# The opening of a two-block transformer kernel: x's tiles loaded back to back, the band matrix in halves, and another order of the pool products

## The chip, the core and the metric

One core of one Trainium2 chip runs the whole program. The metric is the device time of one execution in microseconds, as the median of several executions. Three executions of the kernel before are shown. One further execution of it was profiled.

## The reference, cut to what matters

The model takes 256 tokens of width 1024 through two blocks in float32. The change touches only the very first step of it:

```python
h = rms_norm(x, norm_mix[0])
x = x + pool_mixer(h, pool_w[0], pool_scale[0])
h = rms_norm(x, norm_ffn[0])
x = x + swiglu(h, ffn_w_gate[0], ffn_w_up[0], ffn_w_down[0])
...
```

The pool mixer takes, in each of four groups of 256 columns, the mean over the last 2, 4, 8 or 16 tokens less the token itself, multiplies it by that group's 256x256 matrix of pool_w, and scales the columns by pool_scale. Behind it come a gated feed-forward net (FFN), an attention layer with its own FFN, and a second, longer block. None of these is edited.

## The kernel before, in words

**Layout.** Tokens lie on partitions in two tiles of 128 (t = 0, 1), the width of 1024 in eight slices of 128 (k = 0 to 7). A product that has to be exact to float32 is made from three faster ones: each operand is split into a high part (rounded to float32r, made by ScalarE) and a low part (what is left, made by VectorE as value minus high part), and TensorE sums high by high, high by low and low by high. Weight blocks go round through three buffers, `raw` as loaded, `wh` high and `wl` low.

**Engines.** The program is written by hand, one instruction stream per engine, with semaphores between them. There is no scheduler: each stream runs strictly in the order of the code. SyncE (SP) issues nearly all DMAs, on one queue. GpSimd (POOL) makes the small reciprocal roots and issues a few DMAs much later (cw1, L1785, then cw2, the small bsc and others behind it on its queue; the last gain, L1824, alone).

**The opening, stage by stage.**
- SP issues x's first tile (L526), the band matrix (L528), pool_scale (L529), x's second tile (L526), the table of column gains `col` (L530), pool_w in two halves (L533), `con` and the positions (L535, L536), and then the weights of the FFN (L499).
- TensorE meanwhile multiplies zeros, `WARM_PRODUCTS` = 8 times (L2058, two records each), then spreads pool_scale over all partitions by a product with ones (L2063).
- ScalarE squares x in halves of 512 columns (L722, via `square`), POOL makes the reciprocal root of each tile (L1730, L1731), and VectorE scales the band matrix by it: one instruction for t = 0 (L1265), two for t = 1 (L1269, L1270).
- TensorE makes the pooled and turned activations, all eight slices of t = 0 and then all of t = 1 (L2075). The pooling is itself a product with the band matrix. Three products of zeros follow (`WARM_POOL`, L2081).
- VectorE scales pool_w in two halves (L1279). ScalarE makes the high parts of the turned slices and of pool_w: slices 0, 1, lower half of the weight, slices 2, 3, upper half, slices 4 to 7, then `hi(1)`, the high part of the first FFN block (L731 to L737).
- VectorE makes the low parts: slices 0 to 3 (L1281, recorded at L1091), lower half of the weight (L1283), slices 4 to 7. The low part of the upper half of the weight is POOL's (L1749).
- TensorE's pool products (L2092 to L2115): the lower half's high products, `pool_pass` with xl for both tiles, then with the low weight. For the upper half all three passes of t = 0 come first, then all three of t = 1.
- VectorE adds the four results to x (L1299) in the order n = 0 to 3. Behind n = 1 and n = 2 it makes a quarter of the low part of the first FFN block (`first_quarter`, L1290). The other two quarters come behind `normalise(1)`.
- ScalarE squares the new x (L722), POOL makes the roots, ScalarE scales tile 0 (L616), VectorE tile 1 (L1109), TensorE turns both (L1852) after three more products of zeros (`WARM_BETWEEN`, L2117), and the first product of the FFN begins (`first_up`, L1951).

The order of the work around the change is therefore set by the order of the code on each engine, by the order of SP's one queue, and by the semaphores `x_tile`, `band_loaded`, `pool_scaled`, `t_hi`, `t_lo`, `pool_lo`, `lo_done` and `bank_sum`.

Of the kernel before, what the change touches and what calls it, by code (L numbers as in the profile page):

```python
# [18 lines left out]
ALU = mybir.AluOpType  # L19
AX = mybir.AxisListType  # L20

P = 128
# [44 lines left out]
WARM_PRODUCTS, WARM_POOL, WARM_BETWEEN = 8, 3, 3  # L67
# [44 lines left out]
NBAND = FRONT + NG * EDGE  # L112
NPOOL = FRONT + NG * P


def constants():
# [23 lines left out]
    bands[:, :FRONT] = full[:, :P, :P + EDGE].transpose(1, 0, 2).reshape(P, -1)  # L140
    bands[:, FRONT:] = full[:, P:, P:P + EDGE].transpose(1, 0, 2).reshape(P, -1)
# [94 lines left out]
def build(nc, w, consts, bands, columns_in, positions_in, out):  # L236
# [17 lines left out]
    with ExitStack() as ctx:  # L254
# [147 lines left out]
        con_loaded, band_loaded = sem("con_loaded"), sem("band_loaded")  # L402
# [72 lines left out]
        def _(sp):  # L475
# [93 lines left out]
        def _(act):  # L569
# [150 lines left out]

            def square(q, n, src, t, c):
# [345 lines left out]
        def _(dve):  # L1067
# [192 lines left out]
            def by_group(ap):  # L1260
                return ap.rearrange("p (g c) -> p g c", g=NG)
# [6 lines left out]
            second_tile = by_group(bandr[:, FRONT:NPOOL])  # L1268
            dve.tensor_scalar(second_tile[:, :, 0:EDGE], by_group(band[:, FRONT:NBAND]), rstd[:, 0, 1:2], None, ALU.mult)  # L1269
            dve.tensor_scalar(second_tile[:, :, EDGE:P], by_group(band[:, 0:FRONT])[:, :, EDGE:P], rstd[:, 0, 1:2], None,  # L1270
                              ALU.mult).then_inc(pool_scaled, 1)

# [8 lines left out]
            split_t(0, xh, xl, C_MIX0, 0, range(4))  # L1281
# [3 lines left out]
            split_t(0, xh, xl, C_MIX0, 0, range(4, 8), 4)  # L1285
# [7 lines left out]
            for n, (t, c) in enumerate(((0, 0), (1, 0), (0, 1), (1, 1))):  # L1293
# [424 lines left out]
        def _(pool):  # L1718
# [24 lines left out]

            then(pool.memset(mhalf[:, :], -0.5))

            pool.memset(ksw[:, :, :, :], 0.0).then_inc(ksw_zero, 1)
            inverse_rms(0)
# [84 lines left out]
        def _(pe):  # L1832
# [252 lines left out]
            def pool_pass(half, t, a, b, start=False):  # L2085
                for k in range(4 * half, 4 * half + 4):
# [18 lines left out]

# [488 lines left out]
```

## Time and profile before

| | |
|---|---|
| median of 3 executions | 898.56 us (896.94, 898.56, 898.69) |
| the profiled execution, whole | 898.74 us |
| its span from first to last instruction | 896.8 us |
| TensorE busy | 882.8 us, 98% of the span |
| VectorE busy | 674.3 us, 75% |
| ScalarE busy | 479.6 us, 53% |
| POOL busy | 54.6 us, 6% |
| DMA | 153.47 MB, mean 171 GB/s |

The span leaves out 1.9 us of the profiled execution's own time, before the first and after the last instruction. TensorE is busy nearly all the time, so the time of the whole is TensorE's work plus the few microseconds in which it waits. In the opening, however, part of what TensorE does is multiplying zeros, and there it is a record of busy time that computes nothing.

### The profile page before, as it was taken

What the parts mean: (1) busy time and instruction counts of PE and PEld (TensorE: products, weight loads), DVE (VectorE), ACT (ScalarE), POOL (GpSimd) and SP (SyncE); (2) the same over time, 40 slices, a digit from 0 to 9 for tenths busy, and PEclk for the clock granted to TensorE, in tenths of its full rate; (3) what the DMA queues carried; (4) which work ended last, traced back from release to release, by engine and by line L of the source; (5) the groups of instructions that cost most, each with busy time, mean ns of one, the idle gap of its engine ahead of it and who ended that gap; (6) DMA issues with size and microseconds to landing.
All of it is one profiled execution on the core that took longest, in us unless ns stands there. A gap on an engine that the chain in (4) does not pass through costs nothing.

```text
span 896.8 us, 14483 instructions
## 1 busy us (share of the span) xinstructions
PE 882.8 (98%) x5258; PEld 783.0 (87%) x5258; DVE 674.3 (75%) x1015; ACT 479.6 (53%) x750; POOL 54.6 (6%) x93
## 2 busy tenths in 40 slices
PE   9999999999999999999999999999999899999996
PEld 7888888889998888888888999998998888888885
DVE  5787767778646588677677788896643799999997
ACT  6654444466555665344444645556544665556554
POOL 3300000020000000000000500001100000000000
PEclk9999999999999999999999999999999999999999
DMA  8987666552532768666546684312553566676531
GB/s 248 301 241 210 198 177 186 164 175 84 165 141 94 208 172 255 176 200 197 178 140 211 158 256 156 109 48 73 188 179 101 165 188 187 189 211 185 178 106 47
DMA packets 185574, 153.47 MB, mean 171 GB/s; under 512 B 5089, under 2 KB 170593, under 8 KB 185522
## 3 DMA queue, kind: packets, MB, share of 16 engines
q1 hardware_dynamic: 184770, 150.36, 55.4%
q0 software_dynamic: 752, 2.39, 1.0%
q8 instruction: 35, 0.57, 0.3%
q14 instruction: 17, 0.14, 0.1%
HBM read 151.17 MB, written 1.05 MB: 170 GB/s over the span
## 4 chain that ended last, share of the span: by engine, by line
PE 92%; ACT 3%; DVE 3%; issue 1%; POOLq 0%; POOL 0%; ACTq 0%; DVEq 0%
PE bank L1980 26%; PE bank L1986 13%; PE bank L1835 13%; PE bank L1837 13%; PE bank L1836 13%; PE bank L1951 2%; PE bank L1852 2%; PE bank L1940 1%; DVE wl L1082 1%; ACT wh L588 1%; PE bank L2325 1%; PE bank L2348 1%; PE bank L2529 1%; PE bank L2058 1%; PE bank L2335 1%
## 5 line engine op out<-in xcount | busy, mean ns | idle before, releaser
L1980 PE MATMUL bank<-xhl,wh 128*128 128x512 f32 x1008 | 240.2, 390 | 0.0
L1980 PEld LDWEIGHTS bank<-xhl,wh 128*128 128x128 f32 x1008 | 188.9, 188 | 40.8
L1986 PEld LDWEIGHTS bank<-xhl,wl 128*128 128x128 f32 x1008 | 129.3, 191 | 4.9
L1986 PE MATMUL bank<-xhl,wl 128*128 128x256 f32 x1008 | 130.6, 283 | 0.0
L1221 DVE TENSOR_TENSOR wl<-raw,wh 128x2048 fp32r<-128x2048 f32 x57 | 130.1, 2282 | 0.2 <-ACT wh L674 0.2
L1082 DVE TENSOR_TENSOR wl<-raw,wh 128x2048 fp32r<-128x2048 f32 (+3 forms) x50 | 104.5, 2099 | 28.4 <-ACT wh L588 28.3
L674 ACT ACTIVATE wh<-raw 128x2048 fp32r<-128x2048 f32 x57 | 108.7, 1907 | 3.3 <-DMA raw<-in_ffn_w_up 3.0
L1837 PE MATMUL bank<-dh,hl 128*128 128x512 f32 x264 | 103.4, 392 | 0.0
L1836 PE MATMUL bank<-dl,hh 128*128 128x512 f32 x264 | 103.1, 390 | 0.0
L1835 PE MATMUL bank<-dh,hh 128*128 128x512 f32 x264 | 102.9, 390 | 0.1
L588 ACT ACTIVATE wh<-raw 128x2048 fp32r<-128x2048 f32 (+3 forms) x51 | 89.5, 1769 | 18.1 <-PE bank L1837 7.2
L1170 DVE TENSOR_REDUCE gs<-bank 128x256 f32<-128x512 f32 x66 | 45.4, 687 | 54.6 <-PE bank L1986 54.6
L1213 DVE TENSOR_TENSOR dl<-draw,dh 128x1024 fp32r<-128x1024 f32 x66 | 80.4, 1219 | 4.3 <-ACT dh L650 4.3
L664 ACT ACTIVATE th<-gs 128x256 f32<-128x256 f32 x44 | 18.4, 419 | 114.5 <-DVE gs L1170 114.5
L689 ACT ACTIVATE hh<-pr 128x256 fp32r<-128x256 f32 x66 | 27.5, 417 | 88.8 <-DVE pr L1198 88.8
L650 ACT ACTIVATE dh<-draw 128x1024 fp32r<-128x1024 f32 x66 | 68.9, 1046 | 0.0
L1837 PEld LDWEIGHTS bank<-dh,hl 128*128 128x128 f32 x264 | 49.5, 188 | 10.3
L1835 PEld LDWEIGHTS bank<-dh,hh 128*128 128x128 f32 x264 | 49.8, 189 | 8.7 <-issue 0.5
L1836 PEld LDWEIGHTS bank<-dl,hh 128*128 128x128 f32 x264 | 49.5, 188 | 8.2
L1730 POOL TENSOR_SCALAR st<-ss 128x1 f32<-128x1 f32 x18 | 9.5, 528 | 710.6 <-ACT junk L607 513.3
L1835 PE MATMUL bank<-wh,xhl 128*128 128x512 f32 (+3 forms) x136 | 47.7, 351 | 0.9 <-DVE wl L1082 0.9
L1206 DVE TENSOR_TENSOR hl<-pr,hh 128x256 fp32r<-128x256 f32 x66 | 27.9, 423 | 27.3 <-ACT hh L689 27.3
(331 smaller groups left out, 1555.5 us busy)
## 6 DMA issues: line engine op xcount, KB each, us to landing
raw<-in_ffn_w_up SPq DMA_DIRECT2D x88, 512.0 KB, 6.0
draw<-in_ffn_w_down SPq DMA_DIRECT2D x66, 512.0 KB, 3.6
raw<-in_ffn_w_gate SPq DMA_DIRECT2D x44, 512.0 KB, 5.2
raw<-in_w_in SPq DMA_DIRECT2D x16, 512.0 KB, 5.5
raw<-in_mla_w_o SPq DMA_DIRECT2D x8, 512.0 KB, 3.6
raw<-in_xattn_wv SPq DMA_DIRECT2D x8, 512.0 KB, 4.7
raw<-in_w_out SPq DMA_DIRECT2D x8, 512.0 KB, 4.3
raw<-in_xattn_wq SPq DMA_DIRECT2D x8, 512.0 KB, 5.1
```

Of the source, the lines that this page charges most:

```text
L588: ins = act.activation(h, r, ACT.Copy)
L650: act.activation(dh[s][:, :], draw[s][:, :], ACT.Copy).then_inc(d_hi, 1)
L674: act.activation(wh[ns][:, :], raw[ns][:, :], ACT.Copy).then_inc(hi_done, 1)
L1082: ins = dve.tensor_tensor(l, r, h.bitcast(F32), ALU.subtract)
L1170: dve.tensor_reduce(gs[:, :], gate[:, :].rearrange("p (a s) -> p s a", a=2), AX.X, ALU.add) \
L1213: dve.tensor_tensor(dl[s][:, :], draw[s][:, :], dh[s][:, :].bitcast(F32), ALU.subtract) \
L1221: dve.tensor_tensor(wl[ns][:, :], raw[ns][:, :], wh[ns][:, :].bitcast(F32), ALU.subtract).then_inc(lo_done, 1)
L1835: pe.matmul(outp, a_hi, b_hi, start=start, stop=False, **kw)
L1836: pe.matmul(outp, a_hi, b_lo, start=False, stop=False, **kw)
L1837: return pe.matmul(outp, a_lo, b_hi, start=False, stop=stop, **kw)
L1980: pe.matmul(banks[half][:, :].rearrange("p (a s) -> p a s", a=2), wh[ns][:, a:a + P], xhl[:, :, k, :], start=k == 0, stop=False, skip_grou ...
L1986: ins = pe.matmul(banks[half][:, 0:SEQ], wl[ns][:, a:a + P], xh[:, k, :], start=False, stop=k == KD - 1, skip_group_check=True)
```

## The change

x's second tile is issued right behind the first, then the band matrix in two halves (each with its columns of both token tiles) under two semaphores. pool_scale is loaded by POOL's queue, ahead of POOL's first instruction. `col` goes between the halves of pool_w. ScalarE squares each tile of x in one instruction of 1024 columns and writes the unused squares into `gain`. POOL adds only one sum per tile. VectorE scales the band by halves. TensorE waits per half, multiplies zeros 7 and 2 times where it was 8 and 3, and takes the pool products in another order. VectorE makes the low parts of slices 0, 1, then of the lower half of the weight, then of slices 2 to 7, and moves three of the four quarters between the last addition and `normalise(1)`.

```diff
-WARM_PRODUCTS, WARM_POOL, WARM_BETWEEN = 8, 3, 3
+WARM_PRODUCTS, WARM_POOL, WARM_BETWEEN = 7, 2, 3
...
             for t in range(NT):
                 sp.dma_start(xt[:, t, :], x_dram[:, t, :]).then_inc(x_tile[t], 16)
-                if t == 0:
-                    sp.dma_start(band[:, :], bands).then_inc(band_loaded, 16)
-                    sp.dma_start(pscale[:, :], w["pool_scale"][0:1, :]).then_inc(pscale_loaded, 16)
-            sp.dma_start(col[:, :], columns_in).then_inc(col_loaded, 16)
+            for half in range(2):
+                part = slice(half * BAND_HALF, (half + 1) * BAND_HALF)
+                sp.dma_start(band[:, part], bands[:, part]).then_inc(band_loaded[half], 16)
             for i, (v, (ks, cs_), src) in enumerate(blocks[0][2]):
                 sp.dma_start(v(raw[0])[:, ks, cs_], src).then_inc(pool_part[i], 16)
+                if i == 0:
+                    sp.dma_start(col[:, :], columns_in).then_inc(col_loaded, 16)
...
+            for t in range(NT):
+                act.wait_ge(x_tile[t], 16)
+                if t:
+                    act.wait_ge(sq_done, 2 * t)
+                act.activation(gain[:, :], xt[:, t, :], ACT.Square, scale=ROOT_D, accum_out=ss[:, 0, t, 0:1]) \
+                   .then_inc(sq_done, 2)
...
-            for t in range(NT):
-                act.wait_ge(x_tile[t], 16)
-                for c in range(2):
-                    square(0, 2 * t + c, xt, t, c)
...
-                act.wait_ge(pool_scaled, 3 + half)
+                act.wait_ge(pool_scaled, 2 * NT + half + 1)
...
-            dve.wait_ge(band_loaded, 16)
             dve.wait_ge(rstd_done, 1)
-            dve.tensor_scalar(bandr[:, 0:FRONT], band[:, 0:FRONT], rstd[:, 0, 0:1], None, ALU.mult).then_inc(pool_scaled, 1)
+            for half in range(2):
+                dve.wait_ge(band_loaded[half], 16)
+                dve.tensor_scalar(bandr[:, half * FRONT // 2:(half + 1) * FRONT // 2], front(half), rstd[:, 0, 0:1], None,
+                                  ALU.mult).then_inc(pool_scaled, 1)
             dve.wait_ge(rstd_done, 2)
...
+            for half in range(2):
+                dve.tensor_scalar(second_tile[:, :, 0:EDGE], by_group(edge), rstd[:, 0, 1:2], None, ALU.mult)
+                dve.tensor_scalar(second_tile[:, :, EDGE:P], by_group(front(half))[:, :, EDGE:P], rstd[:, 0, 1:2], None,
+                                  ALU.mult).then_inc(pool_scaled, 1)
...
-            split_t(0, xh, xl, C_MIX0, 0, range(4))
+            split_t(0, xh, xl, C_MIX0, 0, range(2))
             dve.wait_ge(pool_hi, 1)
             dve.tensor_tensor(wl[0][:, 0:D], raw[0][:, 0:D], wh[0][:, 0:D].bitcast(F32), ALU.subtract) \
                .then_inc(pool_lo, 1)
-            split_t(0, xh, xl, C_MIX0, 0, range(4, 8), 4)
+            split_t(0, xh, xl, C_MIX0, 0, range(2, 8), 2)
...
-                if n in (1, 2):
-                    first_quarter(n - 1).then_inc(first_lo, 1)
+                if n == 1:
+                    first_quarter(0).then_inc(first_lo, 1)
             dve.sem_inc(region_free, 1)
+            for i in range(1, 4):
+                first_quarter(i).then_inc(lo_done if i == 3 else first_lo, 1)
             normalise(1)
-            first_quarter(2).then_inc(first_lo, 1)
-            first_quarter(3).then_inc(lo_done, 1)
...
+            pool.dma_start(pscale[:, :], w["pool_scale"][0:1, :]).then_inc(pscale_loaded, 16)
             then(pool.memset(mhalf[:, :], -0.5))
...
-                pe.wait_ge(pool_scaled, t + 1)
                 for k in range(KD):
+                    if k % 4 == 0:
+                        pe.wait_ge(pool_scaled, 2 * t + k // 4 + 1)
...
+            pe.wait_ge(t_lo, 2)
+            for t in range(NT):
+                pool_pass(0, t, xl, h_, ks=range(0, 2))
+            pe.wait_ge(pool_lo, 1)
+            for t in range(NT):
+                pool_pass(0, t, xh, l_)
             pe.wait_ge(t_lo, 4)
             for t in range(NT):
-                pool_pass(0, t, xl, h_)
-            pe.wait_ge(pool_lo, 1)
-            for t in range(NT):
-                pool_pass(0, t, xh, l_).then_inc(bank_sum, 1)
+                pool_pass(0, t, xl, h_, ks=range(2, 4)).then_inc(bank_sum, 1)
...
-            pe.wait_ge(t_hi, 8)
             pe.wait_ge(hi_done, 1)
-            for t in range(NT):
-                pool_pass(1, t, xh, h_, True)
-                if t == 0:
-                    pe.wait_ge(t_lo, 8)
-                pool_pass(1, t, xl, h_)
-                if t == 0:
-                    pe.wait_ge(lo_done, 1)
+            for k in range(4, 8):
+                pe.wait_ge(t_hi, k + 1)
+                for t in range(NT):
+                    pool_pass(1, t, xh, h_, k == 4, range(k - 4, k - 3))
+            for k in (0, 2):
+                pe.wait_ge(t_lo, 6 + k)
+                for t in range(NT):
+                    pool_pass(1, t, xl, h_, ks=range(k, k + 2))
+            pe.wait_ge(lo_done, 1)
+            for t in range(NT):
                 pool_pass(1, t, xh, l_).then_inc((bank_sum, block_used)[t], 1)
```

The number of products that compute something, their shapes and the bytes loaded are the same before and after.

## Rows read from the trace of the kernel before

**Rows 1.** Page, part 4: shares of the chain that ended last, by engine.
```profile
PE 92%; ACT 3%; DVE 3%; issue 1%; POOLq 0%; POOL 0%; ACTq 0%; DVEq 0%
```

**Rows 2.** Chain of waits in order of time, 0 to 32 us: start, us, what.
```profile
1.34 6.47 PE bank L2058 x16
7.81 1.91 PE bank L2063 x4
9.72 2.62 PE bank L2075 x20
...
13.26 0.94 ACT wh L735
...
14.97 0.88 DVE xhl L1091 x2
15.84 1.13 DVE wl L1283
16.98 1.57 DVE xhl L1091 x4
18.55 1.20 DVE x_tok L1299 x2
19.74 0.60 DVE wl L1290
...
21.54 0.68 DVE x_tok L1299
...
22.96 0.62 ACT xn L616
...
23.72 2.06 PE bank L1852 x16
...
25.78 5.98 PE bank L1951 x48
```

**Rows 3.** Weight loads of L2058: min/median/max ns, first and last start.
```profile
L2058 PEld LDWEIGHTS bank<-s x16: 190/337/337, 1.3 to 7.2; 128*128 128x128 f32 x16
```

**Rows 4.** Timeline of TensorE: the last three records of L2058.
```profile
7.00 0.81 PE L2058 MATMUL bank<-s 128*128 128x256 f32 x3
```

**Rows 5.** Timeline, 0 to 26 us: start, us, engine, line, what [idle before].
```profile
0.80 0.11 POOL L1744 MEMSET mhalf<- 128x16 f32 x1 [0.29 <-POOLq L2574]
...
7.80 0.63 ACT L722 ACTIVATE junk<-x_tok 128x512 f32<-128x512 f32 x1 [1.79 <-DMA x_tok<-in_x]
...
10.88 2.34 DVE L1279 TENSOR_TENSOR raw<-raw,bank 128x1024 f32<-128x1024 f32 x2
...
15.76 1.58 ACT L625 ACTIVATE xhl<-bank,col 128x256 fp32r<-128x256 f32 x4
...
15.96 3.28 POOL L1749 TENSOR_TENSOR wl<-raw,wh 128x1024 fp32r<-128x1024 f32 x1 [5.64 <-ACT wh L735]
...
17.19 1.96 ACT L588 ACTIVATE wh<-raw 128x2048 fp32r<-128x2048 f32 x1
...
19.30 0.54 PEld L2088 LDWEIGHTS bank<-wl,xhl 128*128 128x128 f32 x4 [0.16 <-POOL wl L1749]
...
24.03 0.91 DVE L1109 TENSOR_SCALAR xn<-x_tok,rstd 128x512 f32<-128x512 f32 x2 [1.82 <-POOL rstd L1731]
```

**Rows 6.** DMA issues at 2.1 us: x's second tile (KB, us to landing).
```profile
x_tok<-in_x SPq DMA_DIRECT2D x1, 512.0 KB, 5.7
```

**Rows 7.** DMA issues of POOL: the shortest and the smallest (KB, us to landing).
```profile
gain<-in_final_norm_g POOLq DMA_DIRECT2D x1, 512.0 KB, 4.9
...
bsc<-in_gmlp_bs POOLq DMA_DIRECT2D x1, 2.0 KB, 7.1
```

**Rows 8.** Windows, TensorE alone: length, PE busy (records), clock, DMA share, GB/s.
```profile
22.79:23.69 0.90, 0.00 (x0) 1.00 1.12 298
...
700.66:703.00 2.34, 0.02 (x1) 1.00 0.53 93
703.03:706.13 3.10, 3.10 (x16) 0.54 1.02 373
```

More of the change, by code:

```diff
@@ L112 @@
 NBAND = FRONT + NG * EDGE
+BAND_HALF = NBAND // 2
 NPOOL = FRONT + NG * P
@@ L139, in constants @@
             full[g, tok, tok] -= 1.0
-    bands[:, :FRONT] = full[:, :P, :P + EDGE].transpose(1, 0, 2).reshape(P, -1)
-    bands[:, FRONT:] = full[:, P:, P:P + EDGE].transpose(1, 0, 2).reshape(P, -1)
+    for half in range(2):
+        gs_ = slice(2 * half, 2 * half + 2)
+        b = half * BAND_HALF
+        bands[:, b:b + FRONT // 2] = full[gs_, :P, :P + EDGE].transpose(1, 0, 2).reshape(P, -1)
+        bands[:, b + FRONT // 2:b + BAND_HALF] = full[gs_, P:, P:P + EDGE].transpose(1, 0, 2).reshape(P, -1)
     assert np.array_equal(full[:, P:, P + EDGE:], full[:, :P, EDGE:P])
@@ L401, in build @@
         pool_part, pool_hi, pool_lo = [sem("pool_part0"), sem("pool_part1")], sem("pool_hi"), sem("pool_lo")
-        con_loaded, band_loaded = sem("con_loaded"), sem("band_loaded")
+        con_loaded, band_loaded = sem("con_loaded"), [sem("band_loaded0"), sem("band_loaded1")]
         mem_loaded, pscale_loaded = sem("mem_loaded"), sem("pscale_loaded")
@@ L1260, in by_group, with front @@
             def by_group(ap):
-                return ap.rearrange("p (g c) -> p g c", g=NG)
-            dve.wait_ge(band_loaded, 16)
+                return ap.rearrange("p (g c) -> p g c", g=NG // 2)
+            def front(half):
+                return band[:, half * BAND_HALF:half * BAND_HALF + FRONT // 2]
             dve.wait_ge(rstd_done, 1)
-            dve.tensor_scalar(bandr[:, 0:FRONT], band[:, 0:FRONT], rstd[:, 0, 0:1], None, ALU.mult).then_inc(pool_scaled, 1)
+            for half in range(2):
+                dve.wait_ge(band_loaded[half], 16)
+                dve.tensor_scalar(bandr[:, half * FRONT // 2:(half + 1) * FRONT // 2], front(half), rstd[:, 0, 0:1], None,
+                                  ALU.mult).then_inc(pool_scaled, 1)
             dve.wait_ge(rstd_done, 2)
[L1268 to L1271, printed above, removed]
+            for half in range(2):
+                second_tile = by_group(bandr[:, FRONT + half * 2 * P:FRONT + (half + 1) * 2 * P])
+                edge = band[:, half * BAND_HALF + FRONT // 2:(half + 1) * BAND_HALF]
+                dve.tensor_scalar(second_tile[:, :, 0:EDGE], by_group(edge), rstd[:, 0, 1:2], None, ALU.mult)
+                dve.tensor_scalar(second_tile[:, :, EDGE:P], by_group(front(half))[:, :, EDGE:P], rstd[:, 0, 1:2], None,
+                                  ALU.mult).then_inc(pool_scaled, 1)
             dve.wait_ge(scale_spread, 1)
@@ L1742, in inverse_rms_after_norm @@
                     pool.tensor_tensor(rstd[:, 6, one], st2[:, 6, one], r, ALU.mult).then_inc(rstd_done, 1)
+            pool.dma_start(pscale[:, :], w["pool_scale"][0:1, :]).then_inc(pscale_loaded, 16)
             then(pool.memset(mhalf[:, :], -0.5))
             pool.memset(ksw[:, :, :, :], 0.0).then_inc(ksw_zero, 1)
-            inverse_rms(0)
+            for t in range(NT):
+                one = slice(t, t + 1)
+                pool.wait_ge(sq_done, 2 * t + 2)
+                then(pool.tensor_scalar(st1[:, 0, one], ss[:, 0, t, 0:1], EPS, None, ALU.add))
+                pool.tensor_tensor(rstd[:, 0, one], st1[:, 0, one], mhalf[:, 0:1], ALU.pow).then_inc(rstd_done, 1)
             pool.wait_ge(hi_done, 1)
@@ L2083, in _, with pool_pass @@
             h_, l_ = k_view(wh[0], 2 * NG, 256), k_view(wl[0], 2 * NG, 256)
-            def pool_pass(half, t, a, b, start=False):
-                for k in range(4 * half, 4 * half + 4):
+            def pool_pass(half, t, a, b, start=False, ks=range(4)):
+                for k in range(4 * half + ks[0], 4 * half + ks[-1] + 1):
                     o = (k // 2 % 2) * 256
@@ L2098, in _ @@
                               stop=True, skip_group_check=True)
+            pe.wait_ge(t_lo, 2)
[4 more added lines that the diff above has]
+                pool_pass(0, t, xh, l_)
             pe.wait_ge(t_lo, 4)
             for t in range(NT):
-                pool_pass(0, t, xl, h_)
-            pe.wait_ge(pool_lo, 1)
-            for t in range(NT):
-                pool_pass(0, t, xh, l_).then_inc(bank_sum, 1)
-            pe.wait_ge(t_hi, 8)
-            pe.wait_ge(hi_done, 1)
-            for t in range(NT):
-                pool_pass(1, t, xh, h_, True)
-                if t == 0:
-                    pe.wait_ge(t_lo, 8)
-                pool_pass(1, t, xl, h_)
-                if t == 0:
-                    pe.wait_ge(lo_done, 1)
+                pool_pass(0, t, xl, h_, ks=range(2, 4)).then_inc(bank_sum, 1)
+            pe.wait_ge(hi_done, 1)
+            for k in range(4, 8):
[7 more added lines that the diff above has]
+            pe.wait_ge(lo_done, 1)
+            for t in range(NT):
                 pool_pass(1, t, xh, l_).then_inc((bank_sum, block_used)[t], 1)
```

## The prediction

> **What bounds the kernel now.** I read the page's shares of the chain first: TensorE carries 92% of it [rows 1], so behind the opening the time is TensorE's own work and a microsecond won in the opening arrives at the end undiminished, as long as the first FFN steps don't starve. Then the chain of waits for the opening [rows 2], where the reader should see three links. First TensorE bounds itself: warm products 6.47 us, pool_scale's spread 1.91, pooling products from 9.72, the twentieth record of which (t = 1, k = 1) ends at 12.34 and releases ScalarE. Then VectorE: low parts from 14.97, weight half at 15.84, four more low parts from 16.98, the additions from 18.55 with two FFN quarters between them, the last addition from 21.54. Then norm, turn at 23.72, FFN product at 25.78. The timeline [rows 5] shows what stood beside it: x's second tile landed at 7.80, and VectorE, after the bands of both tiles, reached the pool weight at 10.88. None of these is in the chain, since TensorE reached the pooling only at 9.72.
>
> **The change, part by part.**
>
> *Loads.* x's second tile was issued at 2.10 and took 5.7 us [rows 6]. Right behind the first it is two issues earlier and has no longer the band's 320 KB (128 x 640 floats) before it, so it comes earlier by something between 0 and 3 us (its way should not fall under half of 5.7); I take the middle, 1.5 us: landing near 6.3. That is on the path of nothing: tile 1 is needed by TensorE only one tile (half of 32 records at 0.13 us, 2.62/20 from [rows 2], so 2.1 us) after the pooling starts. Worth 0. If this cover went, tile 1 would be late by at most the 1.5 us. The band now lands behind both tiles; by the same shift near 7 us for the first half and a little later for the second, against a need at 9.3 (below). Cost 0, covered by 2 us. The pool weight's first half has `col` behind it instead of before it, so nothing is later there.
>
> *Squares of x, roots, band by halves.* One square for two can only bring tile 0's root forward; VectorE gets six short instructions in place of three. All of it ends before TensorE is through with the spread. Worth 0, cost 0. For VectorE itself: tile 1's bands would be done about 9.5, the weight's scaling (2.34 us for both halves [rows 5]) then waits for the spread at 9.3 and for the landing of the weight, and ends near 12.5, before slices 0 and 1 arrive.
>
> *pool_scale by POOL's queue.* It is issued at about 0.8, where POOL's first instruction of its own stood [rows 5], and TensorE wants it at 7.4. The nearest rows are POOL's later issues, 4.9 us the shortest and 7.1 us for the smallest [rows 7]: landing between 5.7 and 7.9. At 5.7 it costs 0, at 7.9 it costs 0.5. I take 0, because the 7.1 us one stood behind the large load of L1785 in its own queue and this one stands behind nothing; 0.5 stays in the range. On POOL it stands before two memsets, and behind those is the root of tile 0, which waits for a tile of x and its square; the spread at 7.4 covers that too. The Trainium skill (DMA: Bandwidth & Descriptors, "Anatomy of one DMA") gives a fixed 2.0 us to a transfer issued by GpSimd, with which it would land near 3 and rival C would be void; no row here shows one that short.
>
> *One warm product fewer.* The weight loads of the warm products take 337 ns in most records and 190 in the last [rows 3]: TensorE begins at 1.2 GHz and is at 2.4 for the last three records, which start 0.215 us apart ((0.81 - 0.38)/2, [rows 4]). The product removed is two of these, so it is worth **0.43 us**, not the 0.81 that a mean of 6.47/8 would give. The spread ends and the pooling begins at 9.29, the twentieth record ends at 11.91.
>
> *One product of zeros fewer behind the pooling.* The first pool product waits for the lower weight's high part, so this is worth 0; it keeps the zeros from standing in the way once all is 0.43 earlier.
>
> *VectorE's new order.* All in times of before, less 0.43 at the end. VectorE took slices 2 and 3 at 14.97 and the weight half behind them. Now the weight half comes first, as soon as its high part is there, 13.26 + 0.94 = 14.20 [rows 2]: it ends at 15.34 (1.13), slices 2 and 3 at 16.13 (0.79, half of the 1.57 for four). Slices 4 and 5 wait for ScalarE, whose four high parts start at 15.76 and take 1.58 [rows 5]: 16.55, then 17.34 for slices 6 and 7, done at about 18.13. The additions began at 18.55: **0.42 us**, 0.85 with the warm product. So additions 0 and 1 run from 17.70 to 18.90 (1.20 [rows 2]) and the quarter to 19.50 (0.60). Its source, `hi(1)`, is there at 18.7 (17.19 + 1.96 less 0.43).
>
> *TensorE's new order and the third and fourth additions.* The pool weight's last low part is POOL's: 15.96 + 3.28 = 19.24, now 18.81. Before, sixteen products came behind it; now all high and xl products run ahead and eight are left, 0.13 each by four weight loads in 0.54 [rows 5]: four for tile 0, done about 19.4, four for tile 1 by 19.95. The third addition starts at 19.50 for both reasons at once, ends at 20.10, the fourth (its quarter gone) ends at 20.78. It ended at 22.22: 1.44 earlier, which is more than reaches the turn.
>
> *Norm and turn.* ScalarE scales tile 0 once POOL has the root over additions 0 and 2. Addition 2 ended at 20.94 (21.54 less the quarter's 0.60) and now ends at 20.10, so ScalarE's 22.96 [rows 2] goes 0.84 earlier, to 22.1; the fourth square, from 20.8, is over by then. Tile 1's root comes behind tile 0's on POOL, so VectorE's 24.03 moves by at least as much. The three quarters (1.8 us, 20.78 to 22.6) fit in the idle 1.82 us that VectorE had before `normalise(1)` [rows 5]; without that cover they would cost up to 1.8. The turn starts near 22.9 and the FFN near 24.9. **Sum: 0.84 us**, of which 0.43 is the warm product and 0.41 the orders. The span goes from 896.8 to about 896.0, the profiled execution's 898.74 to 897.9, and since that stands 0.18 over the median of the runs shown, the median goes from 898.56 to **897.7**.
>
> **Rivals.** Measurement tells this kernel from no change beyond 0.2%, 1.8 us.
>
> *A, the forecast,* 897.7.
>
> *B, a clock stretch falls out too.* At 700.66 TensorE stood idle for 2.34 us, and its clock was then granted at 0.54 over 16 records that took 3.10 us [rows 8]; the same 16 in the opening took 2.06 [rows 2]. That is 1.04 us of stage time that depends on an idle close to the edge. One of the three executions was 1.6 us below the others, which would fit an execution without it. If the changed kernel is spared, or its first rise to 2.4 GHz comes sooner: 897.7 - 1.04 to 1.6, about 896.4. Against it: the code there is the same and so is the idle.
>
> *C, the opening waits for a load.* pool_scale at 7.9, or the pool weight or `hi(1)` late because their landings don't move with the 0.43: the part before the weight gives nothing, 0.3 to 0.4 of the orders stays, 898.2. That is also the case that the early x tile, the part in the title, does nothing.
>
> *D, slower: the clock falls before the turn.* TensorE ends the pool products near 20.0, the three products of zeros near 21.3, and the turn starts at 22.9: 1.5 us of nothing, where it was 0.90 at a clock that held [rows 8]. At 2.34 it fell. The deciding point lies between. If it falls, the turn's 16 records take 3.10 for 2.06 and the first FFN records lose a little more: 897.7 + 1.04 and some, 898.9, slower than before by 0.3. With pool_scale 0.5 late on top, 899.4. For it: fewer zeros and a longer gap. Against: 1.5 is nearer to 0.90.
>
> **How the numbers follow.** A has 0.57, B 0.19, C 0.11, D 0.13. Faster by over 0.2% means below 896.76: most of B and the edge of A, 0.20. Slower by over 0.2% means above 900.36, which even D doesn't reach with a late load; 0.04. Within: 0.76. The range reaches from B's 896.2 to D's 899.2; past both ends lie some 2 in 10.
>
> **What would show it.** Right: two warm records fewer, the spread starting near 7.3, pooling near 9.3; x's second tile landing before 6.5 with TensorE no earlier for it; VectorE's weight half ahead of slices 2 and 3; the last addition ending near 20.8; FFN at 24.9 +- 0.2, and the rest of the span unchanged. Wrong: TensorE idle between warm products and spread (C), a granted clock under 1 between 21 and 26 us (D), a first FFN step that waits for weights, or a shift at L1951 that is not found again at the end of the span, which would mean that a later stage was bound by loads.

## The result and the profile after

| | before | after |
|---|---|---|
| median | 898.69 us (7 executions, 896.94 to 900.02) | 901.61 us (7 executions, 897.33 to 905.31) |
| ratio | | 1.0034, 95% interval 1.0019 to 1.0049 |
| profiled execution, whole / span | 898.74 / 896.8 us | 900.96 / 899.1 us |
| TensorE busy | 882.8 us | 882.3 us |

The change makes the kernel slower by 0.34% by the ratio, 2.9 us by the medians; the forecast was 897.7, 0.1% faster. A second set of ten executions beside 27 of the kernel before gave 902.13 against 898.64, ratio 1.0035 (1.0020 to 1.0050).

The chain of waits of the changed kernel in order of time (start, us, what), to be laid beside [rows 2]:

```profile
1.34 5.36 PE bank L2077 x14
6.71 1.91 PE bank L2082 x4
8.61 2.62 PE bank L2095 x20
...
15.54 1.66 DVE xhl L1098 x4
17.19 1.20 DVE x_tok L1313 x2
18.39 0.60 DVE wl L1304
18.99 0.61 DVE x_tok L1313
...
19.62 0.73 ACT junk L734 x2
...
20.45 1.03 POOL st L1744
...
21.56 0.86 POOL rstd L1745
...
22.44 0.73 ACT xn L621
...
23.31 3.27 PE bank L1871 x16
26.58 5.75 PE bank L1970 x48
```

The opening is ahead up to the additions. The pooling starts at 8.61 where it was 9.72. The third addition, on which the root of tile 0 hangs, ends at 19.60 (18.99 + 0.61) where it ended at 20.94: 1.34 us ahead. The fourth ends at 20.18, as the timeline below shows (18.90 + 1.28), where it ended at 22.21: 2.0 us ahead. Then the lead melts. Two POOL instructions stand in the chain that were not in it before, and the turn starts at 23.31, only 0.41 ahead of 23.72. Its 16 records take 3.27 us where they took 2.06. The chain puts the FFN at 26.58, 0.80 behind; by the start of the first FFN record it is 26.33 against 25.78, 0.55 behind. The timeline of the same stretch shows why:

```profile
18.90 1.28 DVE L1313 TENSOR_TENSOR x_tok<-bank,x_tok 128x512 f32<-128x512 f32 x2
...
20.10 1.89 DVE L1304 TENSOR_TENSOR wl<-raw,wh 128x512 fp32r<-128x512 f32 x3
...
20.45 1.02 POOL L1744 TENSOR_SCALAR st<-ss 128x1 f32<-128x1 f32 x1 [3.18 <-ACT junk L734]
...
21.56 0.85 POOL L1745 TENSOR_TENSOR rstd<-st,mhalf 128x1 f32<-128x1 f32 x1
...
22.51 0.29 POOL L1744 TENSOR_SCALAR st<-ss 128x1 f32<-128x1 f32 x1
...
22.88 0.55 POOL L1745 TENSOR_TENSOR rstd<-st,mhalf 128x1 f32<-128x1 f32 x1
...
23.31 2.94 PE L1871 MATMUL bank<-con,xn 128*128 128x128 f32 x13 [2.83 <-ACT xn L621]
```

VectorE's three quarters run from 20.10 to 21.99. Beside them POOL's first sum takes 1.02 us and its power 0.85. The same two instructions for the second tile, behind the quarters, take 0.29 and 0.55. Together the roots of tile 0 are 1.03 us longer than those of tile 1. That takes most of the 1.34 us back. And TensorE, which had ended its products early, waits. Windows of 1 us on TensorE alone (length, busy and records, granted clock, DMA share, GB/s), to be laid beside [rows 8]:

```profile
20.00:21.00 1.00, 0.48 (x3) 1.00 0.63 171
21.00:22.00 1.00, 0.00 (x0) 1.00 0.90 253
22.00:23.00 1.00, 0.00 (x0) 0.82 1.09 314
23.00:24.00 1.00, 0.69 (x4) 0.50 1.02 384
...
25.00:26.00 1.00, 1.00 (x7) 0.50 1.05 422
26.00:27.00 1.00, 1.00 (x10) 0.97 1.02 311
```

It has nothing to do from 20.5 to 23.3, 2.83 us. Its granted clock falls to 0.50 (1.2 GHz) just ahead of the turn and stays there until 26. From the turn's first record to the FFN's it is now 3.02 us (26.33 less 23.31) where it was 2.06, so the fall costs 0.96 us here.

So the changed kernel is 0.55 us behind at the FFN, and a lag of 0.5 to 0.6 us is found again at the turns up to 506 us. The other 1.7 to 1.8 us of the span's 2.3 come later. From the turn at 506 us to the one at 610 the changed kernel takes 106.82 us and the kernel before 104.06, and the windows in between show a second fall:

```profile
590.00:595.00 5.00, 5.00 (x43) 1.00 0.02 5
595.00:600.00 5.00, 4.91 (x23) 0.66 0.29 97
600.00:605.00 5.00, 5.00 (x45) 1.00 0.28 114
```

In the kernel before, 595 to 600 us were all at 1.00. A clock of 0.66 over 5 us is 1.7 us of work lost (an estimate: 0.34 of 5.00). Another 0.62 of the 2.76 us is a wait of the turn at 506 us for VectorE, and such differences come without a fall too: in the twelve profiles, of all kernels together, that have none in the 590s, this stage took 104.1 to 105.5 us. One item goes the other way: the fall at 703 [rows 8] is missing from this execution of the changed kernel.

### The profile page after: what moved, and what is told of

Its sections match the earlier page's. It is cut to its first block, busy times and chain, and to the rows that moved or that the text cites. A ratio compares the mean times of both kernels' runs of the same rounds, so it can differ in the third digit from the quotient of the medians.

```text
span 899.1 us, 14475 instructions
## 1 busy us (share of the span) xinstructions
PE 882.3 (98%) x5254; PEld 782.6 (87%) x5254; DVE 675.9 (75%) x1018; ACT 477.9 (53%) x746; POOL 52.3 (6%) x94
## 3 DMA queue, kind: packets, MB, share of 16 engines
HBM read 151.17 MB, written 1.05 MB: 169 GB/s over the span
## 4 chain that ended last, share of the span: by engine, by line
PE 62%; DVE 23%; issue 6%; ACT 5%; DMA 1%; POOL 1%; DVEq 1%; SPq 0%; POOLq 0%; ACTq 0%
PE bank L1999 16%; PE bank L1854 9%; PE bank L1856 9%; PE bank L1855 9%; PE bank L2005 8%; DVE wl L1228 3%; DVE wl L1089 3%; DVE cu L1194 2%; DVE dl L1220 2%; DVE us L1183 2%; ACT wh L593 2%; DVE gs L1177 2%; DVE cg L1194 2%; PE bank L1871 1%; PE bank L1959 1%
```

## Experiments

Two causes are proposed, which the expectations call theories. **P**: POOL's roots run slowly because VectorE's quarters run beside them. **G**: TensorE's clock falls in the gap, the idle time ahead of the turn. The distance from the pooling's first record to the turn's measures the first, the length of the turn and the medians the second.

Each execution comes with its mean granted clock. In the sixteen that were profiled, 0.998 or more meant no fall before the last stage, 0.996 or 0.997 one, and 0.995 or less two or more (in one case one). It is the second thing to read beside each median; it doesn't tell where the falls were. Of 85 executions of the kernel before, run beside the experiments, 46 stood at 0.998 or more and 12 at 0.995 or less, with a median of 898.6 over all. Of 17 executions of the changed kernel one stood at 0.998 (it is the one at 897.33) and 14 at 0.995 or less.

**The changed kernel again.** No edit, for more executions.

> The changed kernel as it is, for more executions on one chip beside the others. Theory G (its clock falls in the idle of 2.8 us ahead of the turn): most executions have a mean clock of 0.995 or less, median 900.5 to 902; the few at 0.998 stand near 897.3. If the 901.6 of seven executions was chance: 898 to 899.

902.13 us (899.64 to 905.06, ten executions), eight of ten at 0.995 or less. Its profile has the same idle, 2.84 us, ahead of a turn of 3.33 us, and falls near 596 and 709 us besides. The slowdown is not chance.

**Quarters behind `normalise(1)`.**

```diff
             dve.sem_inc(region_free, 1)
-            for i in range(1, 4):
-                first_quarter(i).then_inc(lo_done if i == 3 else first_lo, 1)
             normalise(1)
+            for i in range(1, 4):
+                first_quarter(i).then_inc(lo_done if i == 3 else first_lo, 1)
```

> The changed kernel, but the three last quarters stand behind normalise(1) again. Theory P (POOL's two root instructions run slow, 1.02 and 0.86 us against 0.30 and 0.56, because VectorE's quarters run beside them): they take 0.30 and 0.56 again, the turn starts about 1.0 us earlier, near 22.3, TensorE's idle shrinks from 2.8 to 1.8 us. Theory G (it is the fall of TensorE's clock in that idle that costs): by how often the clock still falls at 1.8 us; if it holds, 897 to 898, if it falls as often as before, 900.6. Rival R (the time is lost in later stages whatever the opening does): the median stays within 0.5 of 901.6.

898.63 us (896.94 to 901.85, 11 executions), ratio to before 1.0007 (0.9993 to 1.0021). The timeline:

```profile
20.11 0.30 POOL L1744 TENSOR_SCALAR st<-ss 128x1 f32<-128x1 f32 x1 [3.19 <-ACT junk L734]
...
20.49 0.56 POOL L1745 TENSOR_TENSOR rstd<-st,mhalf 128x1 f32<-128x1 f32 x1
...
21.95 2.06 PE L1871 MATMUL bank<-con,xn 128*128 128x128 f32 x16 [1.66 <-ACT xn L621]
...
22.11 0.92 DVE L1116 TENSOR_SCALAR xn<-x_tok,rstd 128x512 f32<-128x512 f32 x2 [2.27 <-POOL rstd L1745]
```

POOL's instructions are back at 0.30 and 0.56, and the turn starts 13.75 us after the pooling does (21.95 less 8.20) instead of 14.77 (23.31 less 8.54). Theory P holds, for 1.02 us. The idle shrank to about 1.7 us; three of eleven executions are still at 0.995 or less, four stand at 897.06 or less.

**Nine products of zeros ahead of the turn.**

```diff
-WARM_PRODUCTS, WARM_POOL, WARM_BETWEEN = 7, 2, 3
+WARM_PRODUCTS, WARM_POOL, WARM_BETWEEN = 7, 2, 9
```

> The changed kernel with nine products of zeros ahead of the turn where it has three; they end before ScalarE's tile is ready. Theory G: the clock holds through the turn and the first FFN products, the turn takes 2.06 us instead of 3.27, the FFN starts near 25.4, and the median falls to 897.3 to 898.5, as in the one execution of the changed kernel at 897.33 with a mean clock of 0.998. Theory P alone: nothing changes in the turn's start (23.3) and the median stays near 901. Rival R: 901 to 902.

899.33 us (897.58 to 901.45, twelve executions), ratio 1.0011 (0.9999 to 1.0023), one execution of twelve at 0.995. The median is 0.8 above the expected span, but 2.3 to 2.8 below the two medians of the changed kernel. The timeline shows POOL still slow, the distance from pooling to turn still 14.77 us (23.57 less 8.80), and the turn back at 2.07:

```profile
19.28 4.05 PE L2142 MATMUL bank<-s 128*128 128x256 f32 x18
...
20.71 1.02 POOL L1744 TENSOR_SCALAR st<-ss 128x1 f32<-128x1 f32 x1 [3.19 <-ACT junk L734]
...
21.82 0.85 POOL L1745 TENSOR_TENSOR rstd<-st,mhalf 128x1 f32<-128x1 f32 x1
...
23.57 2.07 PE L1871 MATMUL bank<-con,xn 128*128 128x128 f32 x16 [0.24 <-ACT xn L621]
```

So P and G are two causes: the zeros take away the fall in the turn and leave the slow roots, and moving the quarters takes away the slow roots. That edit shortened the idle too, so it doesn't leave G as it was.

**Both edits, seven zeros.**

```diff
-WARM_PRODUCTS, WARM_POOL, WARM_BETWEEN = 7, 2, 3
+WARM_PRODUCTS, WARM_POOL, WARM_BETWEEN = 7, 2, 7
```

> Both edits: quarters behind normalise(1) and seven products of zeros. If P and G are both right, the turn starts near 22.3 at full clock, the FFN at 24.4 against 25.8 in the kernel before: 896.5 to 897.5, below the kernel before and below the run with zeros alone by 1.0. If only G is right, the same as the run with nine zeros. Rival R: 901 to 902.

898.36 us (896.04 to 902.00, twelve), ratio 1.0000 (0.9985 to 1.0014). In the profiled execution the clock first rose late (the warm records took 6.15 us), but the distance from pooling to turn was 13.77 us, and the seven zeros ended at 22.99, just ahead of the turn at 23.10: they delayed nothing. Two of twelve executions stand at 0.995 or less. The four executions at 0.998 or more stand at 896.04, 896.63, 896.79 and 899.18, and the median is not below that of the kernel before. It missed its expectation. Why it is 1 us above the next run, which has one zero less, isn't settled; the intervals of the two overlap.

**Both edits, six zeros.**

```diff
-WARM_PRODUCTS, WARM_POOL, WARM_BETWEEN = 7, 2, 3
+WARM_PRODUCTS, WARM_POOL, WARM_BETWEEN = 7, 2, 6
```

> The changed kernel with the quarters behind normalise(1) and six products of zeros, which should end just before ScalarE's tile is there. Theory G with P: turn at 22.0 at full clock in every execution, median 897.0 to 898.0, at least 1.5 us under the changed kernel and a little under the kernel before; executions at a mean clock of 0.999 near 896.8. Rival R (falls of the clock later in the program decide, and come as often whatever stands ahead of the turn): 898.3 to 899.

897.31 us (896.58 to 898.98, twelve), ratio to the kernel before 0.9989 (0.9979 to 0.9998), and 4.8 us below the changed kernel on the same chip. No execution of twelve at 0.995 or less. The timeline has the zeros and the turn nearly end to end:

```profile
18.84 2.75 PE L2142 MATMUL bank<-s 128*128 128x256 f32 x12
...
22.12 2.06 PE L1871 MATMUL bank<-con,xn 128*128 128x128 f32 x16 [0.53 <-ACT xn L621]
```

This version is ahead of both kernels, of the kernel before only narrowly: 0.11%, with an interval that ends 0.02% short of nothing. The distance from pooling to turn is 13.74 us.

**No zeros in the changed kernel.**

```diff
-WARM_PRODUCTS, WARM_POOL, WARM_BETWEEN = 7, 2, 3
+WARM_PRODUCTS, WARM_POOL, WARM_BETWEEN = 7, 2, 0
```

> The changed kernel without any product of zeros ahead of the turn: idle of about 4.1 us instead of 2.8. Theory G: the clock falls there in every execution, none stands under 899, median 901.5 to 903. If the fall doesn't hang on the idle but on something else in the changed opening: the same 901 as with three zeros, with some executions at 897.3.

902.66 us (901.57 to 905.20, six), ratio 1.0047 (1.0029 to 1.0066), every execution at 0.995 or less, turn 3.60 us after an idle of 4.12. That is what theory G expects.

**No zeros in the kernel before.**

```diff
-WARM_PRODUCTS, WARM_POOL, WARM_BETWEEN = 8, 3, 3
+WARM_PRODUCTS, WARM_POOL, WARM_BETWEEN = 8, 3, 0
```

> The kernel before without its three products of zeros: its idle goes from 0.9 to about 2.2 us and nothing else moves. Theory G: the clock falls ahead of the turn in a part of the executions, median up by 0.5 to 2 us, to 899 to 900.3. If idle of this length is harmless: 898.3, the same.

900.25 us (897.24 to 902.92, twelve), ratio 1.0016 (1.0001 to 1.0031); seven of twelve at 0.995 or less, against 12 of 85 with three zeros. Nothing was changed but the zeros, and with them the idle. In the profiled execution the turn itself ran at full clock,

```profile
22.81 2.06 PE L1852 MATMUL bank<-con,xn 128*128 128x128 f32 x16 [2.24 <-ACT xn L616]
```

and the clock fell later, near 595 and at 704 us. So an idle of 2.24 us ahead of the turn costs 1.6 us in the median, with an interval from 0.1 to 2.8 us by the ratio. In the one execution that was profiled the turn didn't pay for it; whether it did in the others isn't recorded.

**The place of the quarters alone, in the kernel before.**

```diff
-                if n in (1, 2):
-                    first_quarter(n - 1).then_inc(first_lo, 1)
+                if n == 1:
+                    first_quarter(0).then_inc(first_lo, 1)
             dve.sem_inc(region_free, 1)
+            for i in range(1, 4):
+                first_quarter(i).then_inc(lo_done if i == 3 else first_lo, 1)
             normalise(1)
-            first_quarter(2).then_inc(first_lo, 1)
-            first_quarter(3).then_inc(lo_done, 1)
```

> The kernel before with nothing but the change's place for the quarters. Theory P: the last addition ends 0.6 us earlier, POOL's roots are slower by 1.0 us together, the turn starts 0.3 to 1.0 us later than 23.7 and the idle grows from 0.9 to about 2.4; with G on top, the clock falls in a part of the executions: 899.5 to 901. If neither, 898.1 (0.6 us gained).

899.16 us (897.80 to 903.03, twelve), ratio 1.0015 (1.0002 to 1.0027). The turn came later: 14.48 us after the pooling instead of 14.07. The last addition did not come 0.6 us earlier, as expected. It ended 12.55 us after the pooling's start, as in the kernel before (12.56), since with its quarter gone it waited 0.57 us for TensorE.

```profile
21.89 0.30 POOL L1730 TENSOR_SCALAR st<-ss 128x1 f32<-128x1 f32 x1 [2.55 <-ACT junk L722]
...
22.27 1.05 POOL L1731 TENSOR_TENSOR rstd<-st,mhalf 128x1 f32<-128x1 f32 x1
...
23.42 0.85 POOL L1730 TENSOR_SCALAR st<-ss 128x1 f32<-128x1 f32 x1
...
24.23 2.36 PE L1852 MATMUL bank<-con,xn 128*128 128x128 f32 x16 [1.35 <-ACT xn L616]
```

Here it is the power that overlaps (1.05), then the second tile's sum (0.85), and the turn's second half waits for that root. The idle ahead of the turn was 1.35 us and not 2.4, and two of twelve executions stand at 0.995 or less. So the place of the quarters is worth 0.41 us here, and its price depends on what it falls together with.

**Long idle in the best opening.**

```diff
-WARM_PRODUCTS, WARM_POOL, WARM_BETWEEN = 7, 2, 6
+WARM_PRODUCTS, WARM_POOL, WARM_BETWEEN = 7, 2, 0
```

> The version with the quarters behind normalise(1), but without any product of zeros: its opening is the best one's, its idle ahead of the turn about 3.1 us. Of the changed kernel's loss 1.2 us lie in the turn; the rest was a second fall of the clock near 590 to 600 us, in three profiles of three with a fall before the turn and in one of eleven without. If a long idle before the turn brings the later fall with it (theory G2): both falls in the profile, most executions at a mean clock of 0.995 or less, median 900 to 902, 3 us or more above the version with six zeros. If the later fall belongs to the place of the quarters: only the turn's fall, 1.2 us, median 898.5 to 899.

901.56 us (899.37 to 903.48, twelve), ratio 1.0026 (1.0015 to 1.0037), ten of twelve at 0.995 or less. The turn starts 13.86 us after the pooling, nearly as early as in the best version, and pays:

```profile
22.02 3.47 PE L1871 MATMUL bank<-con,xn 128*128 128x128 f32 x16 [2.95 <-ACT xn L621]
```

That is 4.25 us above the version with six zeros by the medians, 3.3 us by the ratios (1.0026 against 0.9989, on two chips), and six products that compute nothing are all that differs. The stretch from the turn's start to the FFN's grew by 1.16 us, from 2.06 to 3.22; the rest, 2.1 us by the ratios and 3.1 by the medians, lies later. The profiled execution, the fastest of the twelve, had the fall near 704 us but none in the 590s, so the expected pair was not seen here. It also lost 1.0 us at the turn at 201 us, which waited 0.85 for VectorE and did not in the best version. That a long idle costs more later than in the turn is shown by these medians; by what it does so is open. The counts alone don't show later falls, since they include the fall in the turn itself.

**Five zeros in the kernel before.**

```diff
-WARM_PRODUCTS, WARM_POOL, WARM_BETWEEN = 8, 3, 3
+WARM_PRODUCTS, WARM_POOL, WARM_BETWEEN = 8, 3, 5
```

> The kernel before with five products of zeros instead of three: its idle of 0.9 us ahead of the turn goes to 0.5, nothing else moves. If the idle of 0.9 us already brought falls later in the program: fewer executions at 0.997 or less than one in three, median 897.5 to 898. If 0.9 us is harmless: 898.3 to 898.7, the same.

898.88 us (897.53 to 900.38, twelve), ratio 0.9999 (0.9987 to 1.0010), one of twelve at 0.995 or less. The five zeros end 0.1 us ahead of the turn, and not the expected 0.5. So of an idle of 0.94 us nearly all was filled, and nothing was gained: 0.9 us is harmless within 0.1%.

**The terms of the sum.** Four variants of the version with six zeros, one part undone in each, and one execution of each. One execution says little about the whole (898.64, 897.28, 898.40 and 899.77 us), since the clock first rises at another time in each; the distance from the pooling's first record to the turn's leaves that out.

| part undone | distance | against 13.74 |
|---|---|---|
| warm products, 8 and 3 | 14.01 | +0.27 |
| load order, pool_scale on SP | 13.75 | 0 |
| TensorE's order | 14.15 | +0.41 |
| VectorE's order | 14.92 | +1.18 |

```diff
-WARM_PRODUCTS, WARM_POOL, WARM_BETWEEN = 7, 2, 6
+WARM_PRODUCTS, WARM_POOL, WARM_BETWEEN = 8, 3, 6
```

> The version with six zeros and the quarters behind, but eight and three products of zeros in the opening as before. Read by the trace: the last warm records start 0.215 us apart at full clock, so if the step of the prediction holds, the spread starts 0.43 us later than with fourteen records at the same first rise of the clock, and the turn with it. If the loads bound the pooling instead, its start doesn't move. Distance from pooling to turn: 13.7, unchanged.

The warm product lies ahead of the pooling and is not in the distance. Eleven profiles with fourteen warm records took 4.92 to 6.30 us for them, mean 5.61; five with sixteen 5.27 to 6.76, mean 6.25. The difference of 0.64 is consistent with the step's 0.43, but no proof of it: the spread within either group is 1.4 to 1.5 us. The distance was not unchanged, as it was expected to be: the third product of zeros behind the pooling pushed the first pool product back (14.34 - 9.38 = 4.96 us behind the pooling's start, against 12.98 - 8.38 = 4.60).

```diff
-            for t in range(NT):
-                sp.dma_start(xt[:, t, :], x_dram[:, t, :]).then_inc(x_tile[t], 16)
+            sp.dma_start(xt[:, 0, :], x_dram[:, 0, :]).then_inc(x_tile[0], 16)
             for half in range(2):
                 part = slice(half * BAND_HALF, (half + 1) * BAND_HALF)
                 sp.dma_start(band[:, part], bands[:, part]).then_inc(band_loaded[half], 16)
+            sp.dma_start(pscale[:, :], w["pool_scale"][0:1, :]).then_inc(pscale_loaded, 16)
+            sp.dma_start(xt[:, 1, :], x_dram[:, 1, :]).then_inc(x_tile[1], 16)
...
-            pool.dma_start(pscale[:, :], w["pool_scale"][0:1, :]).then_inc(pscale_loaded, 16)
```

> The same version with x's second tile behind the band halves and pool_scale on SP's queue again. If the early tile is worth nothing (the prediction): pooling runs through its 32 records in 4.0 us and the distance from pooling to turn stays at 13.7. If it is worth something once the clock rises early: tile 1's band scaling ends near 11.0, TensorE waits for it by up to 0.5 us where the pooling starts before 8.9, and the distance grows by that. Below the start 6.5 of the spread nothing changes unless pool_scale lands later.

The timeline shows the pooling's records in 4.01 us and tile 1's last band (10.62 + 0.33) just ahead of TensorE's need:

```profile
9.05 4.01 PE L2095 MATMUL bank<-bandr,x_tok 128*128 128x144 f32 x32
...
10.62 0.33 DVE L1285 TENSOR_SCALAR bandr<-band,rstd 128x224 f32<-128x224 f32 x1
```

Where the clock rose earlier, in the kernel before without its zeros, the same late tile did cost TensorE 0.3 us (4.30 for 4.01):

```profile
8.46 4.30 PE L2075 MATMUL bank<-bandr,x_tok 128*128 128x144 f32 x32
...
10.15 0.45 DVE L1270 TENSOR_SCALAR bandr<-band,rstd 128x448 f32<-128x448 f32 x1
```

So the early tile is worth between nothing and 0.3 us, by when the clock rises (a reading of two executions, not a test).

```diff
-            for k in range(4, 8):
-                pe.wait_ge(t_hi, k + 1)
-                for t in range(NT):
-                    pool_pass(1, t, xh, h_, k == 4, range(k - 4, k - 3))
...
+            for t in range(NT):
+                pool_pass(1, t, xh, h_, True)
...
```

> The same version with TensorE's pool products in the order of before. If the new order carries (the prediction: eight products behind POOL's low part instead of sixteen), the last product ends 1.0 us later, the last addition waits for it and ends about 1.0 us later, and the distance from pooling to turn grows by 0.3 to 0.5 at most, since the turn hangs on the third addition. If VectorE is the only bound, the distance stays at 13.7.

Distance +0.41, inside the expected 0.3 to 0.5, but not all of it is the order. The fourth addition waited 0.70 us for TensorE, and TensorE then had its six zeros still to do. ScalarE began to scale tile 0 at 22.15; in the other variants the turn follows that start by 0.86 to 0.87 us, here by 1.04. So 0.17 us is the zeros in the way, and 0.24 is left for the order.

```diff
-            split_t(0, xh, xl, C_MIX0, 0, range(2))
+            split_t(0, xh, xl, C_MIX0, 0, range(4))
...
-            split_t(0, xh, xl, C_MIX0, 0, range(2, 8), 2)
+            split_t(0, xh, xl, C_MIX0, 0, range(4, 8), 4)
```

> The same version with VectorE's low parts in the order of before (slices 0 to 3, weight half, slices 4 to 7). The prediction gives the new order 0.42 us: the first addition would start 0.4 later after the pooling's start (8.9 instead of 8.5 us) and the turn 0.3 to 0.4 later, distance 14.1. If POOL's low part is what bounds the additions anyway: 13.7.

Expected 14.1, measured 14.92. The timeline shows two things the expectation lacked:

```profile
15.79 3.29 POOL L1768 TENSOR_TENSOR wl<-raw,wh 128x1024 fp32r<-128x1024 f32 x1 [8.13 <-ACT wh L742]
...
16.86 1.22 PE L2108 MATMUL bank<-wl,xhl 128*128 128x256 f32 x8 [1.07 <-DVE wl L1297]
...
21.01 1.29 DVE L1313 TENSOR_TENSOR x_tok<-bank,x_tok 128x512 f32<-128x512 f32 x2 [0.75 <-PE bank L2108]
```

TensorE's new order asks for the lower weight's low part early and stands behind it, and POOL's own low part takes 3.29 us beside VectorE's weight half (15.60 to 16.82, two inputs in SBUF). In the changed kernel the weight half is over by 14.36, and the same POOL instruction takes 2.42 beside low parts of the slices that have one input in PSUM:

```profile
14.85 2.42 POOL L1768 TENSOR_TENSOR wl<-raw,wh 128x1024 fp32r<-128x1024 f32 x1 [7.02 <-ACT wh L742]
15.54 1.66 DVE L1098 SCALAR_TENSOR_TENSOR xhl<-bank,col,xhl 128x256 fp32r<-128x256 f32 x4 [0.40 <-ACT xhl L630]
```

The two orders belong together: undone singly they cost 0.41 (0.24 without the zeros in the way) and 1.18, undone together (the kernel before, which also has the third zero product) 0.33.

## Why the prediction was wrong

**The warm product, 0.43 us.** Not shown, and nothing speaks against it: 0.64 over sixteen profiles, with a spread of more than twice that in each group. The profiled pooling came 1.11 us earlier and not 0.43; that spread is wide enough to hold the difference, so a part of the lead is luck of this execution.

**Loads, squares, bands, pool_scale: nothing.** Right. x's second tile was there by 5.72, when its square began without a wait. pool_scale was issued at 1.33, not at 0.8, and landed 4.3 to 5.1 us later in the eleven profiles that load it so, near the lower bound taken from [rows 7]. That was early enough, by only 0.1 us where the clock rose early: 6.23 against the spread at 6.32 in the run with the quarters behind. The Trainium skill (DMA: Bandwidth & Descriptors, "Anatomy of one DMA — SWDGE (gpsimd) path") gives 2.0 us for the fixed part; the traces have more than twice that.

**The orders, 0.41 us.** Near in size: without the slow roots the distance is 13.74 against 14.07, 0.33 us. Counted from the pooling's start the additions began at 8.58, where the forecast has 8.41 (17.70 less 9.29) and the kernel before 8.83. The third ended at 10.99 (10.81 forecast, 11.22 before), the fourth at 11.57 (11.49 forecast, 12.50 before). What is missing is 0.17 us on VectorE, whose slices 4 and 5 waited 0.40 for ScalarE. One term was put at nothing and isn't: the product of zeros removed behind the pooling, worth 0.27 in the new order. And one was not foreseen: POOL's low part shortened from 3.28 to 2.42 us.

**Norm and turn: the step that failed.** It said that the three quarters fit in VectorE's idle 1.82 us before `normalise(1)`, and moved POOL's roots by 0.84 us with their old durations. They do fit, for VectorE. But that idle was VectorE waiting for POOL's roots, and the quarters now run beside these. So the term that the prediction put at nothing, the quarters in that idle, measured 1.0 us: the sum and the power take 1.02 for 0.30 and 0.85 for 0.56, and the quarters behind `normalise(1)` bring the turn 1.02 us closer to the pooling again. That the quarters contend is what the Trainium skill (SBUF — State Buffer, "Who interferes with whom") says: a VectorE instruction with two inputs in SBUF contends with a GpSimd instruction that reads SBUF. The quarters subtract one SBUF tile from another, and the sum and the power read SBUF. The trace agrees, with 1.02 beside the quarters and 0.29 without. POOL's low part agrees too, with 3.29 us beside the weight half and 2.42 beside instructions that have one input in PSUM. The kernel before showed only the longer one, 3.28 [rows 5], beside the weight half at 15.84 [rows 2], so its rows held a hint but no proof.

**Rival D, given 0.13, is what happened,** with a bigger gap than it reckoned. It put the idle ahead of the turn at 1.5 us, between 0.90 that held and 2.34 that fell [rows 8]. It was 2.83. With the quarters behind `normalise(1)` it was 1.66, so the estimate was near and the slow roots made the difference. Its price for the turn, 1.04 us "and some", was near too: 0.96 in the changed kernel. What it lacked was that such an idle costs again later, which the prediction put at nothing: the range ended at 899.2 since only one fall was priced. By the runs, idle filled against idle left is worth 3.3 us by the ratios and 4.25 by the medians, of which 1.16 are in the turn. In the profiled execution the terms add up: a span of 896.0 was forecast and 899.1 measured, 3.1 us more. Of these 1.02 are the slow roots, 0.96 the turn at the low clock, 1.75 what came behind the FFN's start and 0.08 the orders, and the early pooling takes off 0.68.

The idle and the turn in this table are from one profile each (two for the changed kernel), the counts from all executions.

| kernel | idle ahead of the turn, us | turn, us | executions at 0.995 or less |
|---|---|---|---|
| before, five zeros | 0.1 | 2.06 | 1 of 12 |
| both edits, seven zeros | 0.1 | 2.06 | 2 of 12 |
| changed, nine zeros | 0.24 | 2.07 | 1 of 12 |
| best version, six zeros | 0.53 | 2.06 | 0 of 12 |
| before | 0.94 | 2.06 | 12 of 85 |
| before, quarters moved | 1.35 | 2.36 (a wait in it) | 2 of 12 |
| changed, quarters behind | 1.66 | 2.06 | 3 of 11 |
| before, no zeros | 2.24 | 2.06 | 7 of 12 |
| changed | 2.83 and 2.84 | 3.27 and 3.33 | 14 of 17 |
| best opening, no zeros | 2.95 | 3.47 | 10 of 12 |
| changed, no zeros | 4.12 | 3.60 | 6 of 6 |

**A, the forecast,** met only one of seventeen executions, 897.33 at a clock of 0.998, and that one is no proof of its sum: the slow roots are in all four profiles that have the quarters in this place, and the kernel before, too, has executions near 897 at 0.998 and more. The signs it named say the same: the spread started at 6.7 and the pooling at 8.6, earlier than its 7.3 and 9.3, but the last addition ended at 20.2 (20.8 forecast) and the FFN began at 26.3 and not at 24.9, and a granted clock under 1 between 21 and 26 us was its sign for D.

**What stays open.** Why a long idle at 22 us costs time hundreds of microseconds later. The two profiles of the changed kernel and the one of its variant without zeros show a fall in the 590s; of the thirteen others only the kernel before without zeros does. A long idle in front of the turn comes with it in four cases, but the best opening with no zeros had none there in the one execution that was profiled. The fall near 703 us comes with short idles as well, the kernel before among them.

## What to carry to other kernels

Where work is moved into an engine's idle time, ask what that idle was waiting for: if it waits for POOL, VectorE work with two SBUF inputs put there slows the very instruction it waits for. When the engine that bounds the kernel gets done sooner but its next work does not, the gap can be a cost of its own (here 0.9 us was harmless within 0.1%, 2.2 us cost 1.6 in the median and 2.9 us cost 3 to 4); fill it with products of zeros that end just before the work arrives, and count them again after every change of what stands on either side. And compare kernels by many executions with their granted clock beside them: here the changed kernel's fastest execution, 897.33, lies below the median of the kernel before.

## What the runs showed of the hardware that was not expected

An idle of 2.24 us raised the share of executions at 0.995 or less from 12 in 85 to 7 in 12; in the one that was profiled the turn behind it took its 2.06 us, and the clock fell near 595 and 704 us. The clock's first rise from 1.2 to 2.4 GHz came at another time in each profile: fourteen warm records took between 4.92 and 6.30 us. (The column of the granted clock stands at 1.00 in those first microseconds too; the rise is read from the records, whose weight loads go from 337 to 190 ns.) The Trainium skill (TensorE: Matmul & The Clock Gate, "What's actually happening") says that this differs from run to run and is not a count of products, and the traces agree. In the profile of the changed kernel the clock fell just behind 596 us although TensorE was idle for only 0.1 us from 590 to 600 (busy 5.00 and 4.91 of 5.00). It had just run narrow products, 16 of 30 columns and 8 of 64; the kernel before ran the same ones from 592.3 to 595.1 us with no fall.
